# A zero fill behind every two gathers of the expert stages, and 12 diagonals in place of 14

## The reference

```python
def block(xb):                                   # xb: 128 x 1024
    q = (xb @ wq).reshape(PEER_BLOCK, PEER_HEADS, 2, PEER_HALF)
    s1 = jnp.einsum('phd,kd->phk', q[:, :, 0], k1).astype(jnp.float32)
    s2 = jnp.einsum('phd,kd->phk', q[:, :, 1], k2).astype(jnp.float32)
    v1, i1 = lax.top_k(s1, PEER_TOPK)            # 16 of 128, twice
    v2, i2 = lax.top_k(s2, PEER_TOPK)
    ...                                          # 16 x 16 sums and their expert numbers
    top_s, top_pos = lax.top_k(cand, PEER_TOPK)
    eid = jnp.take_along_axis(cand_id, top_pos, axis=-1)
    g = jax.nn.softmax(top_s, axis=-1)
    ue = u_tab[eid]                              # a row of 1024 per position, head and pick
    ve = v_tab[eid]
    act = jax.nn.gelu(jnp.einsum('pd,phkd->phk', xb, ue))
    return jnp.einsum('phk,phkd->pd', g.astype(xb.dtype) * act, ve)
```

## Time and profile before

| | us |
|---|---|
| median of 3 runs (3957.39 to 3965.59) | 3965.23 |
| the profiled execution's own time | 3969.06 |
| its span, first to last instruction | 3967.3 |
| PE busy | 3320.0 (84%) |
| DVE busy | 2040.7 (51%) |
| POOL busy | 1031.0 (26%) |
| POOL DMA_INDIRECT, U rows x512 | 485.2 |
| POOL DMA_INDIRECT, V rows x512 | 488.3 |

### The profile page before, as it was taken

The page is one execution under the profiler, slowest core; times in us unless marked ns, Lnnn a source line. Parts: engine busy times, 40 slices in busy tenths (PEclk is TensorE's granted clock), DMA queues, the critical chain, the costliest instruction groups (busy, mean ns, idle before and its releaser), DMA issues. The chain is left out here.

```text
span 3967.3 us, 33939 instructions
## 1 busy us (share of the span) xinstructions
PE 3320.0 (84%) x12000; PEld 2185.2 (55%) x12000; DVE 2040.7 (51%) x3682; ACT 926.2 (23%) x1557; POOL 1031.0 (26%) x1090
## 2 busy tenths in 40 slices
PE   5896577778887577777998999999998988999798
PEld 3663222223663222223876787875687878654387
DVE  5567766654547766655534545433455435302254
ACT  0211111110112111112422434302443312101143
POOL 0026777763016777764000000000000001100000
PEclk9799899999899899999998999998999989999899
DMA  9379999998449999996541555541455533343353
GB/s 365 135 263 383 409 409 409 409 395 329 178 166 383 409 409 409 409 406 262 191 162 64 169 184 167 175 149 64 162 188 165 181 127 108 102 163 107 127 180 116
DMA packets 402037, 951.13 MB, mean 240 GB/s; under 512 B 30652, under 2 KB 171488, under 8 KB 401632
## 3 DMA queue, kind: packets, MB, share of 16 engines
q0 software_dynamic: 147456, 536.94, 34.2%
q1 hardware_dynamic: 245088, 397.09, 29.4%
q10 hardware_dynamic: 9344, 15.22, 1.1%
HBM read 948.06 MB, written 1.07 MB: 239 GB/s over the span
## 5 line engine op out<-in xcount | busy, mean ns | idle before, releaser
L1395 PE MATMUL PS<-v_rows,xn 128*128 128x512 f32 x1944 | 911.0, 612 | 372.6 <-DMA v_rows<-in_peer_v_dram,peer_ids 368.2
L1395 PEld LDWEIGHTS PS<-v_rows,xn 128*128 128x128 f32 x1944 | 355.9, 193 | 926.5 <-issue 592.4
L1470 DVE CUSTOM_DVE_ANT_0 u_rows<-u_rows,PS 128x1024 f32<-128x1024 f32 x512 | 621.8, 1220 | 358.6 <-DMA u_rows<-in_peer_u_dram,peer_ids 330.7
L702 DVE TENSOR_TENSOR ring_lo<-ring,ring_hi 128x2048 fp32r<-128x2048 f32 x198 | 452.8, 2292 | 260.3 <-ACT ring_hi L641 259.8
L1534 POOL DMA_INDIRECT u_rows<-in_peer_u_dram,peer_ids x512 | 485.2, 948 | 281.8 <-issue 145.7
L1534 POOL DMA_INDIRECT v_rows<-in_peer_v_dram,peer_ids x512 | 488.3, 954 | 166.8 <-issue 143.9
L641 ACT CAST ring_hi<-ring 128x2048 fp32r<-128x2048 f32 x198 | 376.8, 1912 | 287.4 <-PE PS L558 156.2
L558 PE MATMUL PS<-ring_hi,hT_hi 128*128 128x512 f32 x1056 | 421.2, 399 | 16.4 <-DVE hT_lo L742 12.1
L440 PE MATMUL PS<-hT,ring 128*128 128x256 f32 x1920 | 423.4, 382 | 2.7 <-PEq L347 1.5
L558 PE MATMUL PS<-ring_hi,hT_lo 128*128 128x512 f32 x1056 | 414.9, 393 | 0.0
L558 PE MATMUL PS<-ring_lo,hT_hi 128*128 128x512 f32 x1056 | 414.8, 393 | 0.0
(11 more groups left out here) (366 smaller groups left out, 2898.4 us busy)
## 6 DMA issues: line engine op xcount, KB each, us to landing
ring<-in_ffn_w_gate_dram SPq DMA_DIRECT2D x132, 512.0 KB, 3.7
ring<-in_ffn_w_up_dram SPq DMA_DIRECT2D x132, 512.0 KB, 4.7
ring<-in_ffn_w_down_dram SPq DMA_DIRECT2D x66, 1024.0 KB, 4.9
ring<-in_w_in_dram SPq DMA_DIRECT2D x64, 1024.0 KB, 4.9
ada_ring<-in_ada_w_dram SPq DMA_DIRECT2D x96, 512.0 KB, 8.2
ring<-in_peer_wq_dram SPq DMA_DIRECT2D x16, 1024.0 KB, 5.2
ring<-in_c_w_in_dram SPq DMA_DIRECT2D x14, 1024.0 KB, 4.9
ring<-in_w_out_dram SPq DMA_DIRECT2D x8, 1024.0 KB, 11.1
```

The source lines that it names most:

```text
L702: nc.vector.tensor_tensor(halves(c)[1], slot, halves(c)[0], ALU.subtract).then_inc(S.w_lo, 1)
L1395: ins = nc.tensor.matmul(self.PS[:, 2 * b + h, :], diag[:, r % NDIAG, :], rowsV[:, m % VRING, h * BANK:(h + 1) * BANK], start=(n % (slots ...
L1470: ins = nc.vector.tensor_tensor_reduce(rowsU[:, m % URING, :], rowsU[:, m % URING, :], H[b], 1.0, 0.0, ALU.mult, ALU.add, dots[:, e:e + 1])
```

## The change

After every two gathers GpSimd writes zeros into 256 columns of `xn` (`pace`) with one `memset`. The memset increments the new semaphore `paced`, and each memset waits until the one before it has been counted; no drain stands behind it. Nothing reads these columns. They take the place of two diagonals: `NDIAG` goes from 14 to 12, and the ring of diagonals starts 256 columns later. The last instruction of GpSimd in the stage waits for all memsets. Per stage there are 256 gather pairs, so 256 memsets; 512 in the program.

```diff
-NDIAG = 14
+NDIAG = 12
...
-                diag = spare[:, 2 * P:].rearrange("p (d n) -> p d n", n=P)
+                pace = spare[:, 2 * P:4 * P]
+                diag = spare[:, 4 * P:].rearrange("p (d n) -> p d n", n=P)
...
-                    def gather_u(n):
+                    def gather_u(n, v):
...
                         for i in range(2):
                             gather(n + i, "peer_u", rowsU, URING, self.u_landed)
-
-                    def gather_v(n):
+                        pause(n // 2 + v // 2)
+
+                    def pause(count):
+
+                        if count > 0:
+                            pool.wait_ge(S.paced, count)
+                        nc.gpsimd.memset(pace, 0.0).then_inc(S.paced, 1)
+
+                    def gather_v(n, u):
...
                         for i in range(2):
                             gather(n + i, "peer_v", rowsV, VRING, self.v_landed)
+                        pause(u // 2 + n // 2)
...
-                        gather_v(v)
+                        gather_v(v, slots)
+                    pool.wait_ge(S.paced, slots)
```

More of the change, by code:

```diff
@@ L1317, in peer @@
                     "n_ms n_rstd n_xn n_tr n_hT p_free0 p_free1 back keysT keysT_out half scores score_out "
-                    "queries shifted expd ids dots gelu weights diag tail", f"peer_q{l}") as (block, S):
+                    "queries shifted expd ids dots gelu weights diag tail paced", f"peer_q{l}") as (block, S):
                 QT = self.sb("peer_qT", [P, 2, LISTS, SEQ], ctx=ctx)
@@ L1560, in _ @@
                     for n in range(0, slots, 2):
-                        gather_u(n)
+                        gather_u(n, v)
                         if n + 2 >= start[item_of[v]] + TOPK * work[item_of[v]][2] + VLAG:
-                            gather_v(v)
+                            gather_v(v, n + 2)
                             v += 2
                     for v in range(v, slots, 2):
-                        gather_v(v)
+                        gather_v(v, slots)
+                    pool.wait_ge(S.paced, slots)
     def pool_conv(self):
```

## The result

| | before | changed |
|---|---|---|
| median, us | 3964.39 (4 runs, 3957.39 to 3965.59) | 4020.11 (4 runs, 4011.63 to 4026.45) |
| profiled execution's own time | 3969.06 | 4014.67 |
| its span | 3967.3 | 4012.9 |

The ratio is 1.0140 with a 95% interval of 1.0119 to 1.0162: 1.4% slower, 55.7 us by the medians, where 66 us had been forecast. The forecast time of 4031 us is 11 us above the median.

The account below looks back on a forecast made before the run. The prediction took the DMA engines at 409 GB/s to bound the expert stages, with POOL bounding them after the change. Two stages at +33.1 us added 66.2 us to 3969.06, so 4035.3, or 4031 for the median; range 3954 to 4130.

Parts of the forecast that it names:

- POOL ahead of the DMA by 0.078 us a pair: Expert stages: two gathers take POOL 2.486 us and the DMA engines 2.564 us, so POOL leads by only 0.078 us.
- The size of a: What one memset with its wait and increment adds to POOL's time per gather pair: 0.26 us, between 0.03 and 0.88.
- the 0.30 us of issue: Time on POOL's timeline in front of each gather's 0.94 us record, although nothing is waited for.
- Rival A: The fill hides in the issue time before a gather, the DMA bounds as before: 3965 give or take 8; chance 0.18.
- 24.7 us of slack: POOL's waits between a stage's 43rd and last gather: 607.7 us of stretch against 583.0 us for 469 steps.
- The row of 12.0 us for ids: POOL's profiled wait for ids, cited with those for used rows and the tail as agreeing with the slack.
- the break-even: Price per pair below which the memset is hidden: 24.7 us over 234 pair steps, 0.106 us.
- The end, 3.0 us back: After a stage's last gather: last row lands after about 4.3 us instead of at most 7.5, returning some 3 us.
- The start and the memset's own wait, taken as 0: 21 more memsets before 334 us are covered by POOL's wait for ids; each memset's wait is already done: both 0.
- 12 diagonals at 0 because V rows land sooner: Two diagonals fewer cost up to 5.1 us a stage, covered because V rows land some 10 us sooner: 0.
- The sum: Per stage +36.1 us of stretch less 3.0 at the end, +33.1; two stages +66.2 us.

Follow-up runs that it names:

- e4: Changed kernel (12 diagonals) with the memset 1 column wide instead of 256; 3974.43 us beside 3961.95 for the kernel before, ratio 1.0026.
- e1: Kernel before with 12 diagonals instead of 14 and no memset; 3979.22 us beside 3961.95, ratio 1.0038.
- e2: Changed kernel with 14 diagonals instead of 12, its 256-column memset written over the key table; 4017.86 us, ratio 1.0138 to the kernel before.
- e3: Changed kernel (12 diagonals) with the memset 128 columns wide instead of 256; 3975.61 us beside 3961.95 for the kernel before, ratio 1.0031.
- e12: Changed kernel with 14 diagonals and a memset of 128 columns over the key table; 3970.99 us beside 3964.25 for the kernel before, ratio 1.0017.
- e8: Kernel before once more, no edit, on chip 12; 3964.36 us.
- e6: Kernel before with 18 diagonals instead of 14 and no memset, on chip 0; ratio 0.9987 to the kernel before, which takes 4131.36 us there.

## Why the forecast was right, point by point

- **POOL ahead of the DMA by 0.078 us a pair, so a small price decides.** Right, and shown by the sweep: with 12 diagonals 1 and 128 columns make the same stretch (613.8 and 614.0 us), 256 make 635.2; and by chip 0, where the stretches of the kernel with two memsets are 29 and 30 us longer than without, instead of 84 and 83.
- **The size of a.** Taken as 0.26 us, measured as 0.191. The slope was near (1.04 ns a column taken, 0.83 measured between 128 and 256 columns); what was missed is that the start of the memset and about the first 25 columns (0.191 - 256 x 0.00083 = -0.021 us) are hidden in the 0.30 us of issue. Rival A was right on the place and wrong on the amount. On 234 steps the 0.069 us are 16.1 us a stage: the largest error of the sum.
- **24.7 us of slack.** Mis-sized: it had taken everything over 469 x 1.243 us for waits. Of it 5.6 us are gathers whose records are longer than 0.938 us (15 of them over 1.0), and these don't go away; they are 7.6 us in the changed kernel. The row of 12.0 us for ids, which the prediction said agrees, holds the 6.58 us ahead of the stretch. The waits are 607.7 - 583.0 - 5.6 = 19.1 us, the break-even 0.082 us. With it the stage comes out: 583.0 + 234 x 0.191 + 7.6 = 635.3 us, measured 635.2.
- **The end, 3.0 us back.** Measured 0.4 (12.4 to 12.0 us). The prediction had set its upper bound of 7.5 us against the shortest landing of all, 4.3. The last gather of the first stage landed 6.4 us after its issue before and 6.1 us after the change: the queue was already short at the end.
- **The start and the memset's own wait, taken as 0.** Right: from the first to the 43rd gather it is 75.8 and 75.9 us before and 75.9 twice after, and one column with its wait and increment added nothing (e4).
- **12 diagonals at 0 because V rows land sooner.** Wrong. In the changed kernel VectorE's wait is

```profile
901.34 0.18 DVE L1460 TENSOR_TENSOR xn<-xn,peer_gates 128x16 f32<-128x16 f32 x1 [21.53 <-ACT xn L1440]
```

  a full round longer, and with 14 diagonals and the same short queue it is 16.3 us. How soon a row lands after its issue has no part in it. What hides most of it is that GpSimd is the bound: it waits only 1.7 + 0.3 = 2.0 us for used rows in the first stage (above). Alone it costs 5.3 and 3.8 us of stretch (e1).
- **The sum.** Forecast +33.1 us a stage, measured +27.5 and +28.8 in the stretches. The price too high by 16.1 us is nearly made up by 5.6 + 2.0 us of long records and by 2.6 at the end that doesn't come back, so the total is closer than its terms, and that is luck. What makes single gathers longer (up to 1.8 us) was not tried. Their sum scatters between executions, 5.6 to 7.5 us a stage in the two profiles of the kernel before, 7.6 to 12.0 in the two of the changed kernel and 5.8 and 6.2 in e2, so that the change makes more of them is not shown.

## What to carry to other kernels

Work beside a saturated resource is free only up to the difference of the two rates. Work both out per item, from start to start, before adding anything to the engine that feeds it, and subtract from the slack what isn't waiting. Slowing a feeder so that its queue stays short gave nothing by itself: with 128 columns the landing time fell from 14.5 to some 6 us and the time did not. (On chip 0 the start of a stage was shorter with two memsets; what did that is open.) When one program runs on two chips, compare stage by stage: there a small difference in the total hid two large ones. And look for a short ring in the wait of the engine behind it: two diagonals fewer made VectorE's wait for the gelu 21.5 us instead of 16.4. The longer ring brought it down to 6.1 us and moved the stall to the next ring.

## What the runs showed of the hardware

- A GpSimd memset of one column between two gathers costs nothing (spacing 2.485 against 2.486 us), of 128 columns 0.085 and 0.091 (e3, e12), of 256 0.191 and 0.198 us (two profiles); its record (0.12, 0.22, 0.33 us) is none of these. Two memsets of 256 columns start 0.25 us apart with records of 0.34.
- Gathers of 128 rows of 4 KB ran at 409 GB/s in the first profile and on chip 12 (e8), and at 365 GB/s on chip 0 (e6); the kernel before takes 3964, 3965 and 4131 us on them.
